# Latent queries and keys computed channel-major, with scores in the array's halves

## What is computed

```python
q = (rms_norm_2(c_q, mla_q_norm[i]) @ mla_w_uq[i]).reshape(B, S, MLA_HEADS, MLA_NOPE + MLA_ROPE)
q = concatenate([q[..., :MLA_NOPE], apply_rope(q[..., MLA_NOPE:], pos)], axis=-1)
kv = (rms_norm_2(c_kv, mla_kv_norm[i]) @ mla_w_ukv[i]).reshape(B, S, MLA_HEADS, MLA_NOPE + MLA_V)
kr = apply_rope(k_rope[:, :, None, :], pos)
mla_k = concatenate([kv[..., :MLA_NOPE], broadcast_to(kr, (B, S, MLA_HEADS, MLA_ROPE))], axis=-1)
mla_v = kv[..., MLA_NOPE:]
...
s = einsum('bqhd,bkhd->bhqk', mla_q, mla_k) * (MLA_NOPE + MLA_ROPE) ** -0.5
pr = softmax(where(causal, s, -inf), axis=-1)
o_mla = einsum('bhqk,bkhd->bqhd', pr, mla_v)
```

## Time and profile before

| | |
|---|---|
| median of three runs | 1026.15 us (1024.49 to 1026.32) |
| the profiled execution | 1025.7 us, its span 1023.8 us |
| mean granted TensorE clock | 0.993 of full speed |
| busy in the span | TensorE 97%, its weight loads 82%, VectorE 60%, ScalarE 49%, GpSimd 2% |
| DMA | 196 MB, 192 GB/s in the mean |

### The profile page before, as it was taken

One profiled execution on the slowest core, in us unless ns is written; L12 is line 12 of the kernel. 1 busy time (PEld: TensorE's weight loads), 2 busy tenths in 40 slices (PEclk: granted clock), 3 DMA queues, 4 the chain that ended last, 5 costly groups with the idle time before them and its releaser, 6 DMA issues.

```text
span 1023.8 us, 13497 instructions
## 1 busy us (share of the span) xinstructions
PE 992.0 (97%) x5626; PEld 837.5 (82%) x5626; DVE 618.1 (60%) x748; ACT 503.9 (49%) x628; POOL 25.0 (2%) x47
## 2 busy tenths in 40 slices
PE   8999899999998999999999999999999999999996
PEld 6665689999987999878888888889987788888885
DVE  5786935444448649865455455664895654545465
ACT  4445365455454547644444444653664644443453
POOL 0000000000000000010000000100000100000010
PEclk9999899999999999999999999999999999999999
DMA  9987886654525443245555456435323555555531
GB/s 334 415 307 278 331 349 234 205 200 165 198 70 193 176 152 130 71 165 206 203 170 203 170 200 221 158 133 201 124 83 125 195 206 170 200 186 185 199 110 41
DMA packets 30934, 196.07 MB, mean 192 GB/s; under 512 B 3731, under 2 KB 5832, under 8 KB 9880
## 3 DMA queue, kind: packets, MB, share of 16 engines
q1 hardware_dynamic: 30874, 195.22, 52.6%
HBM read 194.14 MB, written 2.04 MB: 192 GB/s over the span
## 4 chain that ended last, share of the span: by engine, by line
PE 80%; DVE 12%; issue 3%; ACT 3%; DMA 2%; POOL 0%; SPq 0%; DVEq 0%; POOLq 0%; ACTq 0%
PE ps L1652 56%; PE ps L2007 9%; PE ps L2063 5%; DVE lo L1068 3%; ACT hi L612 1%; DMA scratch<-stream 1%; PE ps L1757 1%; PE ps L2311 1%; PE ps L2193 1%; PE ps L2147 1%; DVE scratch L1444 1%; DMA h<-x 1%; DVE scratch L1510 1%; DVE scratch L1461 1%; PE ps L2214 0%
## 5 line engine op out<-in xcount | busy, mean ns | idle before, releaser
L1068 DVE TENSOR_TENSOR lo<-raw,hi 128x2048 fp32r<-128x2048 f32 (+5 forms) x140 | 310.3, 2219 | 232.1 <-ACT hi L612 232.1
L612 ACT ACTIVATE hi<-raw 128x2048 fp32r<-128x2048 f32 (+4 forms) x140 | 263.8, 1888 | 143.1 <-PE ps L1652 110.1
L1652 PE MATMUL ps<-hi,xh 128*128 128x512 f32 (+2 forms) x704 | 275.1, 391 | 10.0 <-DVE xl L1109 4.4
L1652 PE MATMUL ps<-lo,xh 128*128 128x512 f32 (+2 forms) x704 | 269.2, 382 | 0.0
L1652 PE MATMUL ps<-hi,xl 128*128 128x512 f32 (+2 forms) x704 | 268.9, 382 | 0.0
L1652 PEld LDWEIGHTS ps<-hi,xh 128*128 128x128 f32 x704 | 132.2, 188 | 45.0 <-issue 11.1
L1652 PEld LDWEIGHTS ps<-lo,xh 128*128 128x128 f32 x704 | 132.1, 188 | 25.1
L1652 PEld LDWEIGHTS ps<-hi,xl 128*128 128x128 f32 x704 | 132.4, 188 | 22.6
L1652 PE MATMUL ps<-hi,gh 128*128 128x512 f32 (+2 forms) x328 | 125.2, 382 | 0.0
L1652 PE MATMUL ps<-lo,gh 128*128 128x512 f32 (+2 forms) x328 | 124.6, 380 | 0.0
L1652 PE MATMUL ps<-hi,gl 128*128 128x512 f32 (+2 forms) x328 | 124.5, 380 | 0.0
(11 more groups left out here) (257 smaller groups left out, 1062.8 us busy)
## 6 DMA issues: line engine op xcount, KB each, us to landing
raw<-stream SPq DMA_DIRECT2D x142, 1024.0 KB, 4.8
scratch<-stream SPq DMA_DIRECT2D x22, 1024.0 KB, 8.9
raw<-stream SPq DMA_DIRECT2D x4, 1020.0 KB, 5.0
raw<-stream SPq DMA_DIRECT2D x4, 896.0 KB, 4.9
raw<-stream SPq DMA_DIRECT2D x2, 864.0 KB, 4.5
raw<-stream SPq DMA_DIRECT2D x2, 768.0 KB, 5.1
raw<-stream SPq DMA_DIRECT2D x2, 680.0 KB, 5.1
h<-x SPq DMA_DIRECT2D x2, 512.0 KB, 5.3
```

Of the source, the lines that this page charges most:

```text
L612: nc.scalar.activation(hi[:, u["s"] % SPLIT_SLOTS, 0:n], raw_of(u, n), ACT.Copy).then_inc(S["hi_done"], 1)
L1068: nc.vector.tensor_tensor(lo[:, slot, first:n], raw_of(u, n)[:, first:n], hi[:, slot, first:n].bitcast(F32), ALU.subtract).then_inc(S["lo_ ...
L1652: ins = nc.tensor.matmul(out, l, r, start=start and i == 0, stop=stop and i == 2, skip_group_check=skip)
```

## The change

Of the latent queries and keys, the 64 columns a head that are not rotated are now computed channel-major: `lora_product` makes three tiles of 128 channels (two heads each) with the weights stationary and 256 tokens moving, straight in the layout of `qT` and `kT`. What is left of each product stays token-major: 192 rotated columns of uq, 384 value columns of ukv. The weights' columns are laid out anew for that on the host. Only the rotated part is transposed: `q7` holds per head 32 columns in a field of 64, two heads to a transpose (six transposes), and the rotated key, written twice beside itself, takes two. The copies out of PSUM follow.

A head's scores become a 64-row product and a 32-row product that adds to it. Even heads lie in the upper half of the array's rows and in one pair of banks, odd heads in the lower half and in the other pair. Per block come six 64-row products, six 32-row products and six masks. `latent_scores` and `latent_at` name the new places in PSUM and in the statistics. The order of stages and the semaphores' places on each engine stay as they were; `kv_done` counts two a layer now.

The diff, cut to its core:

```diff
-        kfull = two["Z"][:, 0:NB * HM * QK].rearrange("p (b h d) -> p b h d", b=NB, h=HM)
+        rope_k = two["Z"][:, 0:NB * P].rearrange("p (b h d) -> p b h d", b=NB, h=2)
...
-        q7 = two["Y"][:, 0:NB * 7 * QK].rearrange("p (b h d) -> p b h d", b=NB, h=7)
+        q7 = two["Y"][:, 0:NB * 7 * NOPE].rearrange("p (b h d) -> p b h d", b=NB, h=7)
...
-        qT = two["qT"].rearrange("p (h q) -> p h q", h=HM)
-        kT = two["kT"].rearrange("p (h q) -> p h q", h=HM)
+        qT = two["qT"].rearrange("p (t q) -> p t q", t=6)
+        kT = two["kT"].rearrange("p (t q) -> p t q", t=4)
...
+        def latent_scores(b):
+            banks = ps[:, 0:4, :].rearrange("p (e a) c -> p e (a c)", e=2) if b else ps[:, 4:6, :]
+            return banks[:, :, 0:3 * P * (b + 1)].rearrange("p e (t k) -> p e t k", t=3)
+        def latent_at(b, hh):
+            return HM * b + 3 * (hh % 2) + hh // 2
...
                 product(act, ("uq", layer))
-                for b in range(NB):
-                    nc.scalar.activation(q7[:, b, 0:HM, :].rearrange("p h d -> p (h d)").rearrange("p (a c) -> p a c", a=2),
-                                         ps[:, 2 * b:2 * b + 2, 0:UQ_COLS // 2], ACT.Copy).then_inc(S["q7_done"], 1)
+                nc.scalar.activation(q7[:, :, 0:HM, 0:ROPE], ps[:, 2:4, 0:HM * ROPE].rearrange("p b (h d) -> p b h d", h=HM),
+                                     ACT.Copy).then_inc(S["q7_done"], 1)
+                nc.scalar.activation(qT[:, 0:3, :].rearrange("p t q -> p (t q)"), ps[:, 0:2, :].rearrange("p a c -> p (a c)")[:, 0:3 * SEQ],
+                                     ACT.Copy).then_inc(S["q7_done"], 1)
...
                 act.wait_ge(S["rope_done"], 2 * layer + 2)
-                act.wait_ge(S["kv_done"], 4 * layer + 4)
                 for b in range(NB):
-                    nc.scalar.activation(kfull[:, b, :, NOPE:QK], q7[:, b, HM:HM + 1, NOPE:QK].broadcast_to([P, HM, ROPE]),
+                    nc.scalar.activation(rope_k[:, b, :, 0:ROPE], q7[:, b, HM:HM + 1, 0:ROPE].broadcast_to([P, 2, ROPE]),
...
                 act.wait_ge(S["qkT_ps"], 2 * layer + 1)
-                nc.scalar.activation(qT[0:QK].rearrange("p h q -> p (h q)"), ps[0:QK, 0:3, :].rearrange("p a c -> p (a c)"),
+                nc.scalar.activation(qT[:, 3:6, :].rearrange("p t q -> p (t q)"), ps[:, 2:4, :].rearrange("p a c -> p (a c)")[:, 0:3 * SEQ],
...
                 product(dve, ("ukv", layer))
-                for b in range(NB):
-                    src = ps[:, 2 * b:2 * b + 2, 0:UKV_COLS // 2].rearrange("p a (h d) -> p a h d", h=3)
-                    nc.vector.tensor_copy(mv[:, b, :, :].rearrange("p (a h) d -> p a h d", a=2),
-                                          src[:, :, :, NOPE:NOPE + VD]).then_inc(S["kv_done"], 1)
-                    nc.vector.tensor_copy(kfull[:, b, :, 0:NOPE].rearrange("p (a h) d -> p a h d", a=2),
-                                          src[:, :, :, 0:NOPE]).then_inc(S["kv_done"], 1)
+                nc.vector.tensor_copy(mv.rearrange("p b h d -> p b (h d)"), ps[:, 2:4, 0:HM * VD]).then_inc(S["kv_done"], 1)
+                nc.vector.tensor_copy(kT[:, 0:3, :].rearrange("p t q -> p (t q)"),
+                                      ps[:, 0:2, :].rearrange("p a c -> p (a c)")[:, 0:3 * SEQ]).then_inc(S["kv_done"], 1)
...
                 dve.wait_ge(S["qkT_ps"], 2 * layer + 2)
-                nc.vector.tensor_copy(kT[0:QK].rearrange("p h q -> p (h q)"),
-                                      ps[0:QK, 3:6, :].rearrange("p a c -> p (a c)")).then_inc(S["kT_done"], 1)
+                nc.vector.tensor_copy(kT[:, 3, :], ps[:, 4, 0:SEQ]).then_inc(S["kT_done"], 1)
...
                     dve.wait_ge(S["m_sc"], 2 * layer + i + 1)
-                    src = (ps[:, 0:3, :].rearrange("p a (t k) -> p (a t) k", t=2) if b else
-                           ps[:, 3:5, :].rearrange("p a (t k) -> p (a t) k", t=4)[:, 0:HM, :])
-                    nc.vector.tensor_reduce(row_max[:, HM * b:HM * (b + 1)], src, AX.X, ALU.max).then_inc(S["m_step"], 1)
+                    nc.vector.tensor_reduce(row_max[:, HM * b:HM * (b + 1)].rearrange("p (e t) -> p e t", e=2), latent_scores(b), AX.X, ALU.max).then_inc(S["m_step"], 1)
...
-                def lora_product(stage, cols, k0):
+                def lora_product(stage, k0, cols):
                     u = units_of((stage, layer))[0]
                     wh, wl = parts(u)
+                    for k in range(u["kts"]):
+                        for t_ in range(3):
+                            cs = slice(t_ * P, (t_ + 1) * P)
+                            for i, (a, w) in enumerate(((gh, wh), (gl, wh), (gh, wl))):
+                                nc.tensor.matmul(ps[:, t_ // 2, (t_ % 2) * SEQ:(t_ % 2 + 1) * SEQ], w[:, k, cs], a[:, k0 + k, :],
+                                                 start=(k == 0 and t_ % 2 == 0 and i == 0), stop=(k == u["kts"] - 1 and i == 2),
+                                                 skip_group_check=True)
+                    cs = slice(3 * P, 3 * P + cols)
                     for b in range(NB):
                         sl = slice(b * P, (b + 1) * P)
                         for k in range(u["kts"]):
-                            for i in range(2):
-                                c = slice(i * cols // 2, (i + 1) * cols // 2)
-                                ins = three(ps[:, 2 * b + i, 0:cols // 2], gh[:, k0 + k, sl], gl[:, k0 + k, sl],
-                                            wh[:, k, c], wl[:, k, c], start=k == 0, stop=k == u["kts"] - 1)
+                            ins = three(ps[:, 2 + b, 0:cols], gh[:, k0 + k, sl], gl[:, k0 + k, sl], wh[:, k, cs], wl[:, k, cs],
+                                        start=k == 0, stop=k == u["kts"] - 1)
                     used(ins, u)
...
-                pe.wait_ge(S["kv_done"], 4 * layer + 4)
-                for hh in range(HM):
+                pe.wait_ge(S["kv_done"], 2 * layer + 2)
+                for t_ in range(3):
                     for b in range(NB):
-                        at = hh * SEQ + b * P
-                        ins = nc.tensor.transpose(ps[0:QK, at // 512, at % 512:at % 512 + P], q7[:, b, hh, :], ident)
+                        at = t_ % 2 * SEQ + b * P
+                        ins = nc.tensor.transpose(ps[:, 2 + t_ // 2, at:at + P], q7[:, b, 2 * t_:2 * t_ + 2, :].rearrange("p h d -> p (h d)"), ident)
                 ins.then_inc(S["qkT_ps"], 1)
                 pe.wait_ge(S["kf_done"], 2 * layer + 2)
-
                 pe.wait_ge(S["relu_i"], 2 * layer + 2)
-                for hh in range(HM):
-                    for b in range(NB):
-                        at = hh * SEQ + b * P
-                        ins = nc.tensor.transpose(ps[0:QK, 3 + at // 512, at % 512:at % 512 + P], kfull[:, b, hh, :], ident)
+                for b in range(NB):
+                    ins = nc.tensor.transpose(ps[:, 4, b * P:(b + 1) * P], rope_k[:, b, :, :].rearrange("p h d -> p (h d)"), ident)
                 ins.then_inc(S["qkT_ps"], 1)
...
                     nk = P * (b + 1)
                     for hh in range(HM):
-                        at = hh * nk
-                        bank = (0 if b else 3) + at // 512
-                        nc.tensor.matmul(ps[:, bank, at % 512:at % 512 + nk], qT[0:QK, hh, b * P:(b + 1) * P], kT[0:QK, hh, 0:nk],
-                                         start=True, stop=False, skip_group_check=True)
-                        at += nk - P
-                        ins = nc.tensor.matmul(ps[:, bank, at % 512:at % 512 + P], ident16[:], masks16[:, 0, :],
+                        r = slice(NOPE * (hh % 2), NOPE * (hh % 2) + NOPE)
+                        nc.tensor.matmul(latent_scores(b)[:, hh % 2, hh // 2, :], qT[r, hh // 2, b * P:(b + 1) * P], kT[r, hh // 2, 0:nk],
+                                         start=hh < 2 or (b == 1 and hh > 3), stop=False, skip_group_check=True)
+                    for hh in range(HM):
+                        r = slice(NOPE * (hh % 2), NOPE * (hh % 2) + ROPE)
+                        nc.tensor.matmul(latent_scores(b)[:, hh % 2, hh // 2, :], qT[r, 3 + hh // 2, b * P:(b + 1) * P], kT[r, 3, 0:nk],
+                                         start=False, stop=False, skip_group_check=True)
+                    for hh in range(HM):
+                        ins = nc.tensor.matmul(latent_scores(b)[:, hh % 2, hh // 2, nk - P:nk], ident16[:], masks16[:, 0, :],
                                                start=False, stop=True, skip_group_check=True)
                     ins.then_inc(S["m_sc"], 1)
...
-        put(("uq", layer), 0, g("mla_w_uq_2")[layer])
-        put(("ukv", layer), 0, g("mla_w_ukv_2")[layer])
+        for name, w, width in (("uq", g("mla_w_uq_2")[layer], QK), ("ukv", g("mla_w_ukv_2")[layer], NOPE + VD)):
+            heads = w.reshape(-1, HM, width)
+            put((name, layer), 0, np.concatenate([heads[:, :, :NOPE].reshape(-1, HM * NOPE), heads[:, :, NOPE:].reshape(-1, HM * (width - NOPE))], 1))
```

(31 more changed lines are left out.)

## The result

| | median | runs |
|---|---|---|
| before | 1025.82 us | 22 (1023.71 to 1027.00) |
| changed | 1027.37 us | 22 (1026.11 to 1030.06) |

The account below looks back on a forecast made before the run. TensorE, busy 97% of the span, was taken as the bound. Terms 0.61 + 0 + 0 + 0.20 + 0.14 = 0.95 us a layer, +1.9 us in two, gave 1027.8 us; range 1025.7 to 1031.9.

Parts of the forecast that it names:

- B: Narrow uq products and step to 32-row tiles: no new price, 0.1 to 0.2 us a layer, 1026.2 us; chance 0.22.
- C: Scores: the 32-row products don't share their time in pairs, 3.9 us in all, 1031.7 us; chance 0.12.
- uq: uq product: 36 products become 27 of 256 columns and 18 of 192, all at 0.120 us, +0.61 us a layer.
- rival D: uq's 18 narrow products: price of plain fp32, 0.32 instead of 0.12 us each, 1035.0 us; chance 0.16.
- ukv: ukv product: six more instructions, +0.08 us, ahead of a 0.3 us wait for VectorE, so taken as 0.
- Transposes: Ahead of sb: 24 become 8, 1.75 us less work a layer, replaced by waiting for six ScalarE copies; 0 us.
- Scores: Latent scores split into 64-row and 32-row products: +0.20 us in block 1, +0.14 in block 0, each layer.
- Relief of the other engines: Smaller qT and kT copies, worth 0.7 and 1.3 us: VectorE's gain only lengthens its wait before the row maximum; nothing.

## Why the prediction was right

**The forecast.** 1.9 us more was summed up; 1.6 came. 1027.8 was said and 1027.37 measured. The chances of 0.54 for "within 0.2%" and 0.43 for slower were near even, and the result lies on the line between them. The range, 1025.7 to 1031.9, also took in B and C, so that the time lies in it says little; what bears the forecast out is that each term was found in its place.

**uq: right in kind, too high.** +0.61 was taken, +0.44 came. The floor is the weight load, not the columns, as the run with 128 columns shows, and not the price of plain fp32 (rival D), which would be 0.32 us. But I put the 13 ns of the wider products on top of it, 0.120, where 0.111 was measured: my lower end of 0.105 to 0.120 was nearer. 18 x 0.009 = 0.16 is all but 0.01 of the difference. The load by the Trainium skill, TensorE: Matmul & The Clock Gate, section LDWEIGHTS (loading the stationary operand), 0.107 us for 128 columns, gave +0.38; the trace agrees with it to 4 ns.

**ukv: right.** +0.07 at its end, gone at the next wait for VectorE's low part: the shift is 0.51 at the index scores of block 0 and 0.44 at dsa's first product (373.77 before, 373.22 after).

**Transposes: right, and the step that decides.** A wait of 1.7 us a layer, released by the last of the six copies, was said and is there. The run with the transposes put back shows that their work was free, the run with sb started early that the 1.86 us are to be had once nothing is waited for. What the prediction didn't see was the second engine behind the copies, VectorE's low part, 0.45 us later. It didn't matter to the forecast, but it would have to whoever tried to collect the gain.

**Scores: right.** +0.20 was said for block 1 and +0.21 came (0.63 less 0.42); +0.14 for block 0, and +0.17 came (0.80 less 0.63). The unknown price, from 64-row to 32-row tiles, was taken from the step between the full array and its halves, 0.19, and measured as 0.2 by the run without it. That the two are alike was a guess that came true: none of the rows shown had tiles of 32 rows. The Trainium skill, TensorEngine Tiling (Array Packing), section Key Properties, has a change of tiling mode drain TensorE; this case agrees, also between the two sizes of row tile. Rival C (no pairs of 32 rows) is out by the starts, 12 records in 1.49 us; B (no new price) by both measured prices.

**Relief of the other engines: right.** What VectorE saved turned into idle time ahead of the maximum, 1.98 instead of 0.33 us, of which 0.63 is the later end of the scores.

Not tried: tiles of 32 rows four at a time, and another way of computing the rotated columns of uq than as narrow products. So the +0.44 of uq remains in every version here.

## What to carry to other kernels

Work taken off the busiest engine counts only up to the next thing that engine waits for: look at what ends, on the other engines, while the removed work runs, and at what would end next after that. Here ScalarE's copies ended as the last transpose did, and the 16 transposes removed a layer were worth nothing until the order behind them was changed, then 1.9 us a layer; the new order alone paid 0.2. Splitting a contraction of 96 rows into 64 and 32 to use the array's halves gives nothing, since both parts stream all columns (block 1 took 3.22 us with 96 rows, 3.43 split, and 3.23 split without the change of tile size), and if it must be split, rows of zeros that keep one tile size are cheaper than the change of size.

## What the hardware showed that I had not expected

A narrow fp32r product costs 0.111 us at 192 and at 128 columns, while 256 cost 0.120. So there is a floor of about 0.11 us under products with 128 stationary columns, and nothing dearer below 256 moving ones: the price of plain fp32 (0.32 for 192 columns), to which I gave a chance of 0.16, doesn't exist for these forms. The step from 64-row to 32-row tiles costs the same 0.2 us as that from the full array to its halves. And up to the latent weights' transposes an instruction stream repeats to 0.01 us from a fixed point within the layer, where single executions of the kernel before scatter over 3 us, which made effects of 0.2 us a layer readable. Much of that scatter goes with the granted clock of the first 130 us: over the ten traces the index key transposes of layer 0 start between 346.94 us, where that clock was 1.00, and 351.13, where it was 0.94, though no run changes anything ahead of them; from 143 to 1005 us the clock was 1.00 in all ten.
